# Hybrid diffusion backbone: the second choice of experts ahead of the first lowered piece, and the third piece behind the first hidden product

## Chip, cores, metric

One NeuronCore of a Trainium2 chip runs the whole program. The metric is the device time in microseconds (us), a median over several executions.

## What is computed

Two layers, each with a token mixer (neighbourhood attention, a Mamba-2 scan and a gated MLP) and a channel mixer, for 128 context tokens and 128 latent tokens with D = 1024. The change is in the channel mixer, a hierarchical mixture of experts with 4 groups of 8 experts, of which each token takes one group and two experts of it:

```python
p_coarse = jax.nn.softmax((x @ w_coarse).astype(jnp.float32), -1)
p_g, g_sel = lax.top_k(p_coarse, 1)
fine = (x @ w_fine).astype(jnp.float32).reshape(-1, MOE_GROUPS, MOE_EXPERTS_PER_GROUP)
fine_g = jnp.take_along_axis(fine, g_sel[:, :, None], axis=1)[:, 0]
top_v, top_i = lax.top_k(fine_g, MOE_TOP_K)
w_top = jax.nn.softmax(top_v, -1) * p_g
...
hid = jax.nn.silu(jnp.einsum('td,edf->tef', x, w1)) * jnp.einsum('td,edf->tef', x, w3)
y = jnp.einsum('tef,efd->td', hid * gates[:, :, None], w2)
```

## The kernel before

The five engines run instruction streams written out by hand, each in its own block, and meet at semaphores. An engine works through its stream in order, so the order in the text of a block is the order on the engine. `wait_ge` waits for a semaphore; `tally(ins, sem)` lets an instruction increment one, `drain()` on DVE or ACT is an instruction of the engine's queue that stands for the end of what came before it.

**Weights.** The weights of the experts come as pieces of 128 x 2048 fp32 (1 MB) in the order of `BODY` (line 81): piece 0 and 1 are the halves of `up` (w1 and w3) of expert 0, then for each further expert two pieces `up` and the piece `down` (w2) of the expert before. So piece 2 and 3 are `up` of expert 1, piece 4 is `down` of expert 0. SP loads piece j to slot j % 4 of `raw` once the slot is free (`expert_loads`). Each product is made in three matmuls (`mm3`) from a high and a low part of both factors: ACT copies a piece to `wh` (`convert`, L1691), DVE subtracts it from the piece to `wl` (`lower`, which is called `piece(j)` in the stream, L1792) and thereby gives back the slot. There are three pairs of buffers wh and wl (`PARTS = 3`), given back by TensorE.

**Routing.** From the logits DVE finds the coarse group (`first`, L2355) and the first choice of experts; TensorE counts ranks; DVE makes the selection matrix `selg` of group 0 (`choose(0, 0)`, L2363), which releases the gathers. Then DVE lowers piece 0 (`lower(Tally(dve), 0, 0)`). `finish_routing` finds the second choice, hands it to ACT for an exponential (`rt_in`; `grown(1)` on ACT, L1704), and makes the gates. ACT does the exponential for the group softmax (`grown(0)`) before its loop, and `grown(1)` after it has copied x2 to x2h (L1738).

**Entrance to the loop.** TensorE gathers the tokens of group 0 with 32 matmuls (gather 0 and gather 1, `bank<-selg,x`); ACT takes the high part (`xgh`, L1726) and DVE the low part (`xgl`). `up(0)` is 24 matmuls from `wh`, `wl`, `xgh`, `xgl`: its first half needs piece 0 and gather 0, its second half piece 1 and gather 1. Behind it gather 4 turns selg and picks the gates of the group; for that it waits for `gsel_ready`, the copy of the gates that `weigh` makes on DVE (L2430). DVE then copies the results (`gg`, L2456, `selT`, L2457) and makes `hid` of expert 0 (L2482) with ACT's `sil` (L1748). TensorE turns hid (L920), goes on to `up(1)`, whose first half needs piece 2, gathers a part of group 1 between its halves (this waits for `select(tally, rnd, 1)` on DVE), and does `down(0)` behind it.

**Loop.** For each expert DVE has: hid, piece 3i+3, the low part of the turned hid (`hTTl`), some extra work, pieces 3i+4 and 3i+5. ACT has: sil, piece 3i+3, `hTTh` (L1754), pieces 3i+4 and 3i+5. The order on DVE at the entrance was: gather 0's low part, piece 1, gather 1's low part, `finish_routing`, `weigh`, piece 2, the copies of gather 4.

The whole is done twice, for layer 0 and layer 1 (the entrances are at about 356 and 1011 us). A second round of the loop exists for groups of more than 128 tokens; it did not run here.

Of the kernel before, what the change touches and what calls it, by code (L numbers as in the profile page):

```python
# [342 lines left out]
def hybrid_backbone(nc, A, O):  # L343

    with ExitStack() as ctx:
# [1114 lines left out]
        def _(act):  # L1460
# [30 lines left out]
            for l in range(L):  # L1491
# [209 lines left out]
                def grown(n):  # L1701
                    act.wait_ge(rt_in, 2 * l + n + 1)
                    w = rtr[:, :, 0:4] if n == 0 else rtr[:, :, 40:41]
                    A_(w, w, ACT.Exp).then_inc(rt_exp, 1)  # L1704

                grown(0)

                def begin(tally, rnd):
                    if rnd:
                        convert(tally, rnd, 0)  # L1710

                def stream(tally, rnd, final):
                    def piece(j):
                        if j < len(BODY):
                            convert(tally, rnd, j)

                    def summed(g):
                        for n in range(2):
                            b = SUM_BANK + n
                            act.wait_ge(full[b], loop_uses(b, l, rnd, g + 1 - n))  # L1720
                            tally(A_(ygh[:, n * 512:(n + 1) * 512], bank[b][:, :], ACT.Copy), yg_high)

                    def gathered(g, j):
                        b, n = gather_use(g, j)
                        act.wait_ge(full[b], loop_uses(b, l, rnd, n))
                        ins = A_(xgh[g % 2][:, 4 * j:4 * j + 4, :], bank[b][:, :].rearrange("p (c t) -> p c t", c=4), ACT.Copy)  # L1726
                        if g:
                            ins.then_inc(free[b], 1)
                        tally(act.drain(), xg_act)

                    gathered(0, 0)
                    if rnd:
                        piece(1)
                    gathered(0, 1)
                    piece(2)
                    if rnd == 0:
                        for s in range(2):
                            A_(x2h[:, s, :], x2[:, s, :], ACT.Copy)  # L1738
                            act.drain().then_inc(x2_high, 1)
                        grown(1)  # L1740
                    for i in range(NE):
                        g, e = i // EPG, i % EPG
                        if i == NE - LATE:
                            tally.late = act.mark_branch_hint_location()
                        act.wait_ge(full[UP_BANK], loop_uses(UP_BANK, l, rnd, 1 + i))

                        act.wait_ge(free[UP_BANK], loop_uses(UP_BANK, l, rnd, 1 + i))
                        tally(A_(sil[:, :], bank[UP_BANK][:, 0:FF], ACT.Silu), sil_done)  # L1748
                        piece(3 * i + 3)
                        if i == NE - 1 and final and l < L - 1:  # L1750
                            cut[l + 1] = 0
                            convert_to(l + 1, 0)
                        act.wait_ge(full[TURN_BANK], loop_uses(TURN_BANK, l, rnd, TURN_USE["hidden", i]))
                        tally(A_(hTTh[i == NE - 1][:, :, :], bank[TURN_BANK][:, 0:FF].rearrange("p (c t) -> p c t", c=2), ACT.Copy), hidT_high)  # L1754
                        if i and e == 0:
                            summed(g - 1)
                        piece(3 * i + 4)
                        piece(3 * i + 5)
                        if i + 1 < NE and prepared_at(i + 1):
                            to, j = prepared_at(i + 1)  # L1760
                            if j < 2:
                                gathered(to, j)
                    summed(EG - 1)
                    if final and l < L - 1:
                        convert_to(l + 1, 1)
# [21 lines left out]
        def _(dve):  # L1787
# [81 lines left out]
            for l in range(L):  # L1869
# [472 lines left out]
                def r_(a, b):  # L2342
                    return rtr[:, :, a:b]
# [44 lines left out]
                V.tensor_scalar(place[:, :, 1:2], place[:, :, 0:1], -float(P), None, ALU.add)  # L2388
                bank_full(dve, l, "x211")
                choose(0, 0).then_inc(sel_ready, 1)  # L2390
                lower(Tally(dve), 0, 0)
                def finish_routing():

                    first(24, 8, "rev8", 5)
                    V.scalar_tensor_tensor(out=r_(16, 24), in0=r_(24, 32), scalar=-BIG, in1=r_(16, 24), op0=ALU.mult, op1=ALU.add)
                    drain()
                    V.tensor_reduce(r_(7, 8), r_(16, 24), X, ALU.max)
                    drain()
                    tt(r_(32, 40), r_(16, 24), r_(7, 8).to_broadcast([P, 2, 8]), ALU.is_equal)
                    tt(r_(40, 41), r_(7, 8), r_(6, 7), ALU.subtract)  # L2400
                    drain().then_inc(rt_in, 1)

                    first(32, 8, "rev8", 5)
                    dve.wait_ge(rt_exp, 2 * l + 2)
                    V.tensor_reduce(r_(41, 42), r_(0, 4), X, ALU.add)
                    V.tensor_scalar(r_(42, 43), r_(40, 41), 1.0, None, ALU.add)
                    drain()
                    tt(r_(43, 44), r_(41, 42), r_(42, 43), ALU.mult)
                    drain()
                    V.reciprocal(r_(44, 45), r_(43, 44))  # L2410
                    drain()
                    tt(r_(45, 46), r_(44, 45), r_(40, 41), ALU.mult)
                    drain()
                    tt(r_(24, 32), r_(24, 32), r_(44, 45).to_broadcast([P, 2, 8]), ALU.mult)
                    tt(r_(32, 40), r_(32, 40), r_(45, 46).to_broadcast([P, 2, 8]), ALU.mult)
                    drain()
                    tt(r_(24, 32), r_(24, 32), r_(32, 40), ALU.add)
                    drain()
                    for s in range(2):
                        tt(gates[:, s, :].rearrange("p (g e) -> p g e", g=4), bc(rtr[:, s, 24:32], 1, 4), bc(rtr[:, s, 8:12], 2, 8), ALU.mult)  # L2420
                    drain()

                def begin(tally, rnd):
                    if rnd:
# [12 lines left out]
                def stream(tally, rnd, final, begins=0, ends=NE):  # L2437
                    def piece(j):
                        if j < len(BODY):
                            lower(tally, rnd, j)  # L2440
# [26 lines left out]
                            tally(drain(), yg_low)  # L2467

                    if begins == 0:
                        gathered(0, 0)  # L2470
                        piece(1)
                        gathered(0, 1)
                        if rnd == 0:
                            finish_routing()
                            weigh(tally, 0)
                            piece(2)
                        gathered(0, 4)
                    for i in range(begins, ends):
                        g, e = i // EPG, i % EPG
# [2 lines left out]
                        tally(V.scalar_tensor_tensor(out=hid[:, :], in0=bank[UP_BANK][:, FF:2 * FF], scalar=gg[:, g % 2, e:e + 1],  # L2482
                                                     in1=sil[:, :], op0=ALU.mult, op1=ALU.mult), free[UP_BANK])
                        tally(drain(), hid_ready)
                        if i == 0 and rnd:
                            piece(2)
                        piece(3 * i + 3)
                        dve.wait_ge(full[TURN_BANK], loop_uses(TURN_BANK, l, rnd, TURN_USE["hidden", i]))
# [68 lines left out]
```

## Time and profile before

| | before |
|---|---|
| three runs | 1343.54, 1347.97, 1348.94 us |
| median | 1347.97 us |
| span of the profiled execution | 1351.2 us |
| TensorE busy | 1250.6 us (93%) |
| DVE busy | 1006.3 us (74%) |
| ACT busy | 741.8 us (55%) |
| HBM read | 349.77 MB, 262 GB/s over the span |

All rows come from that one execution of 1351.2 us. Busy shares are averages over stages of different kinds, so the stage in question has to be read by its own rows: who waited for whom there. A row of the timeline gives in brackets how long the engine was idle before the instruction and what ended it; "issue" means that the profile shows nothing it waited for. Matmul ends are modelled; starts are firmer.

### The profile page before, as it was taken

The numbers are of one execution on the slowest core, as the hardware profiler recorded it, in microseconds if no ns is written. First come the engines' busy times: TensorE is split into PE (matmuls) and PEld (weight loads), VectorE is DVE, ScalarE is ACT, GpSimd is POOL, SyncE is SP. The second block draws the span as 40 slices with busy tenths as digits, with TensorE's granted clock in tenths as the row PEclk, the third lists the DMA queues.
The fourth block names the chain that finished last, engine by engine and source line by source line (L and its number), as shares of the span: only waits on it lengthen the run. The fifth ranks groups of instructions, "written<-read, shape, count | busy, mean of one in ns | idle before, by whom it ended". The sixth has DMA issues, their size and how long they took to land.

```text
span 1351.2 us, 16800 instructions
## 1 busy us (share of the span) xinstructions
PE 1250.6 (93%) x6097; PEld 977.0 (72%) x6097; DVE 1006.3 (74%) x1154; ACT 741.8 (55%) x704; POOL 66.8 (5%) x113
## 2 busy tenths in 40 slices
PE   4999999989899999999989999998988999999994
PEld 1767777777676777887757777776777778788773
DVE  0646567787589888888877475768857888888886
ACT  1543453652656667677753345356346566666773
POOL 1400001001000000000020000010000000000000
PEclk8899998989889999999989989998999999999998
DMA  9988654538668989899976767454436898889991
GB/s 357 315 271 312 247 176 138 185 108 327 238 250 315 336 313 344 316 339 343 354 216 206 276 231 268 156 171 149 156 130 225 282 361 324 319 328 337 340 355 56
DMA packets 98092, 353.68 MB, mean 262 GB/s; under 512 B 9060, under 2 KB 12608, under 8 KB 81616
## 3 DMA queue, kind: packets, MB, share of 16 engines
q1 hardware_dynamic: 87504, 295.12, 61.0%
q0 software_dynamic: 10496, 57.39, 12.3%
q8 instruction: 51, 0.84, 0.2%
q14 instruction: 41, 0.34, 0.1%
HBM read 349.77 MB, written 3.74 MB: 262 GB/s over the span
## 4 chain that ended last, share of the span: by engine, by line
PE 60%; DVE 23%; ACT 5%; DMA 5%; issue 3%; DVEq 3%; ACTq 1%; SPq 1%; POOL 0%; POOLq 0%
PE bank L917 56%; DVE wl L1792 13%; PE bank L920 3%; DMA adaw<-in_w_ada 2%; ACT wh L1691 2%; DMA first<-in_w_ada 1%; DVE tmp L1792 1%; ACT wh L1484 1%; DVE merged L1792 1%; DVE hid L2482 1%; DMA decay<-decay_rows 1%; DVE x L1792 1%; ACTq L1579 1%; DMA raw<-in_moe_w 1%; ACT gate L1578 0%
## 5 line engine op out<-in xcount | busy, mean ns | idle before, releaser
L1792 DVE TENSOR_TENSOR wl<-raw,wh 128x2048 fp32r<-128x2048 f32 (+1 forms) x268 | 610.4, 2278 | 126.2 <-ACT wh L1484 78.8
L1691 ACT ACTIVATE wh<-raw 128x2048 fp32r<-128x2048 f32 x192 | 367.6, 1917 | 60.3 <-PE bank L917 50.9
L917 PE MATMUL bank<-wh,xgh 128*128 128x512 f32 x512 | 211.6, 413 | 0.1
L917 PE MATMUL bank<-wh,xgl 128*128 128x512 f32 x512 | 204.3, 399 | 0.0
L917 PE MATMUL bank<-wl,xgh 128*128 128x512 f32 x512 | 203.8, 398 | 0.0
L1484 ACT ACTIVATE wh<-raw 128x2048 fp32r<-128x2048 f32 (+1 forms) x76 | 142.3, 1872 | 103.8 <-PE bank L917 62.7
L917 PE MATMUL bank<-wh,hTh 128*128 128x512 f32 x448 | 186.4, 416 | 6.9 <-DVE wl L1792 4.0
L917 PE MATMUL bank<-wl,hTh 128*128 128x512 f32 x448 | 181.7, 406 | 0.0
L917 PE MATMUL bank<-wh,hTl 128*128 128x512 f32 x448 | 181.0, 404 | 0.0
L917 PEld LDWEIGHTS bank<-wh,xgl 128*128 128x128 f32 x512 | 97.3, 190 | 23.6
L917 PEld LDWEIGHTS bank<-wh,xgh 128*128 128x128 f32 x512 | 98.0, 191 | 20.0 <-issue 0.5
L917 PEld LDWEIGHTS bank<-wl,xgh 128*128 128x128 f32 x512 | 97.9, 191 | 19.7
L917 PEld LDWEIGHTS bank<-wh,hTh 128*128 128x128 f32 x448 | 87.3, 195 | 30.9 <-DVE wl L1792 7.7
L917 PE MATMUL bank<-wh,hTTh 128*128 128x512 f32 x256 | 102.7, 401 | 2.5 <-DVE wl L1792 2.5
L917 PEld LDWEIGHTS bank<-wh,hTl 128*128 128x128 f32 x448 | 87.0, 194 | 21.4
L917 PEld LDWEIGHTS bank<-wl,hTh 128*128 128x128 f32 x448 | 87.5, 195 | 19.4
L917 PE MATMUL bank<-wl,hTTh 128*128 128x512 f32 x256 | 101.5, 396 | 0.0
L917 PE MATMUL bank<-wh,hTTl 128*128 128x512 f32 x256 | 101.3, 396 | 0.0
L1754 ACT ACTIVATE hTTh<-bank 128x256 fp32r<-128x256 f32 x64 | 24.7, 386 | 86.5 <-PE bank L920 86.5
L917 PEld LDWEIGHTS bank<-wh,hTTh 128*128 128x128 f32 x256 | 48.2, 188 | 18.1 <-DVE wl L1792 6.4
L1748 ACT ACTIVATE sil<-bank 128x256 f32<-128x256 f32 x64 | 24.6, 385 | 59.7 <-PE bank L917 59.7
L917 PEld LDWEIGHTS bank<-wh,hTTl 128*128 128x128 f32 x256 | 48.2, 188 | 11.7
(302 smaller groups left out, 1563.6 us busy)
## 6 DMA issues: line engine op xcount, KB each, us to landing
raw<-in_moe_w SPq DMA_DIRECT2D x256, 512.0 KB, 4.7
raw<-in_moe_w SPq DMA_DIRECT2D x64, 1024.0 KB, 5.2
raw<-in_w_in SPq DMA_DIRECT2D x52, 1024.0 KB, 6.1
adaw<-in_w_ada POOLq DMA_DIRECT2D x32, 1024.0 KB, 6.4
raw<-in_w_branch SPq DMA_DIRECT2D x12, 1024.0 KB, 5.2
raw<-in_w_ada SPq DMA_DIRECT2D x8, 1024.0 KB, 10.6
raw<-in_w_o SPq DMA_DIRECT2D x8, 1024.0 KB, 4.8
first<-in_w_ada SPq DMA_DIRECT2D x4, 1024.0 KB, 16.8
```

Source lines behind the costliest of these rows:

```text
L917: return behind(nc.tensor.matmul(*args, **kw))
L920: return behind(nc.tensor.transpose(*args))
L1484: A_(wh[c][:, 0:n], raw[:, r, 0:n], ACT.Copy).then_inc(part_high[c], 1)
L1579: act.drain().then_inc(gate_ready, 1)
L1691: tally(A_(wh[c][:, :], raw[:, r, :], ACT.Copy), part_high[c])
L1748: tally(A_(sil[:, :], bank[UP_BANK][:, 0:FF], ACT.Silu), sil_done)
L1754: tally(A_(hTTh[i == NE - 1][:, :, :], bank[TURN_BANK][:, 0:FF].rearrange("p (c t) -> p c t", c=2), ACT.Copy), hidT_high)
L1792: return V.tensor_tensor(o, a, b, op)
L2482: tally(V.scalar_tensor_tensor(out=hid[:, :], in0=bank[UP_BANK][:, FF:2 * FF], scalar=gg[:, g % 2, e:e + 1], in1=sil[:, :], op0=ALU.mult, ...
```

## The change

The seven operations on DVE that find the second choice leave `finish_routing` and become `second_choice`, which runs before piece 0 is lowered. `grown(1)` on ACT runs directly behind `grown(0)`. In the stream on DVE, piece 1 stands ahead of the low part of gather 0, and piece 2 behind hid of expert 0 (ahead of piece 3), as it already stood in a second round. The operations are the same; none is added or removed.

```diff
--- before.py
+++ after.py
@@ -1704,6 +1704,7 @@
                     A_(w, w, ACT.Exp).then_inc(rt_exp, 1)
 
                 grown(0)
+                grown(1)
 
                 def begin(tally, rnd):
                     if rnd:
@@ -1737,7 +1738,6 @@
                         for s in range(2):
                             A_(x2h[:, s, :], x2[:, s, :], ACT.Copy)
                             act.drain().then_inc(x2_high, 1)
-                        grown(1)
                     for i in range(NE):
                         g, e = i // EPG, i % EPG
                         if i == NE - LATE:
@@ -2388,8 +2388,8 @@
                 V.tensor_scalar(place[:, :, 1:2], place[:, :, 0:1], -float(P), None, ALU.add)
                 bank_full(dve, l, "x211")
                 choose(0, 0).then_inc(sel_ready, 1)
-                lower(Tally(dve), 0, 0)
-                def finish_routing():
+
+                def second_choice():
 
                     first(24, 8, "rev8", 5)
                     V.scalar_tensor_tensor(out=r_(16, 24), in0=r_(24, 32), scalar=-BIG, in1=r_(16, 24), op0=ALU.mult, op1=ALU.add)
@@ -2399,6 +2399,8 @@
                     tt(r_(32, 40), r_(16, 24), r_(7, 8).to_broadcast([P, 2, 8]), ALU.is_equal)
                     tt(r_(40, 41), r_(7, 8), r_(6, 7), ALU.subtract)
                     drain().then_inc(rt_in, 1)
+
+                def finish_routing():
 
                     first(32, 8, "rev8", 5)
                     dve.wait_ge(rt_exp, 2 * l + 2)
@@ -2419,6 +2421,9 @@
                     for s in range(2):
                         tt(gates[:, s, :].rearrange("p (g e) -> p g e", g=4), bc(rtr[:, s, 24:32], 1, 4), bc(rtr[:, s, 8:12], 2, 8), ALU.mult)
                     drain()
+
+                second_choice()
+                lower(Tally(dve), 0, 0)
 
                 def begin(tally, rnd):
                     if rnd:
@@ -2467,13 +2472,12 @@
                             tally(drain(), yg_low)
 
                     if begins == 0:
+                        piece(1)
                         gathered(0, 0)
-                        piece(1)
                         gathered(0, 1)
                         if rnd == 0:
                             finish_routing()
                             weigh(tally, 0)
-                            piece(2)
                         gathered(0, 4)
                     for i in range(begins, ends):
                         g, e = i // EPG, i % EPG
@@ -2482,7 +2486,7 @@
                         tally(V.scalar_tensor_tensor(out=hid[:, :], in0=bank[UP_BANK][:, FF:2 * FF], scalar=gg[:, g % 2, e:e + 1],
                                                      in1=sil[:, :], op0=ALU.mult, op1=ALU.mult), free[UP_BANK])
                         tally(drain(), hid_ready)
-                        if i == 0 and rnd:
+                        if i == 0:
                             piece(2)
                         piece(3 * i + 3)
                         dve.wait_ge(full[TURN_BANK], loop_uses(TURN_BANK, l, rnd, TURN_USE["hidden", i]))
```

## Rows read from the trace of the kernel before

**Rows 1.** The page's chain that ended last, shares of the span by line
```profile
PE bank L917 56%; DVE wl L1792 13%; PE bank L920 3%; DMA adaw<-in_w_ada 2%; ACT wh L1691 2%; DMA first<-in_w_ada 1%; DVE tmp L1792 1%; ACT wh L1484 1%; DVE merged L1792 1%; DVE hid L2482 1%; DMA decay<-decay_rows 1%; DVE x L1792 1%; ACTq L1
```

**Rows 2.** Chain of work from 384 to 446 us, shares by line
```profile
by line: DVE wl L1792 62.9%; DVE x L1792 7.9%; issue 6.9%; DVE hTTl L1792 4.1%; DVE x2l L1792 4.0%; DVE hid L2482 3.9%; ACT wh L1691 3.1%; DVE xgl L2453 2.2%; DVEq L2334 1.3%; DVE selg L2363 0.6%; DVEq L2458 0.5%; DVEq L2492 0.5%; DVEq L236
```

**Rows 3.** Timeline of DVE, layer 0: start us, us, engine, line, op, out<-in, [idle before <-releaser]
```profile
356.00 2.29 DVE L1792 TENSOR_TENSOR wl<-raw,wh 128x2048 fp32r<-128x2048 f32 x1
360.73 0.69 DVE L1792 TENSOR_TENSOR xgl<-bank,xgh 128x512 fp32r<-128x512 f32 x1 [2.43 <-ACTq L1729]
361.55 2.29 DVE L1792 TENSOR_TENSOR wl<-raw,wh 128x2048 fp32r<-128x2048 f32 x1
364.05 0.69 DVE L1792 TENSOR_TENSOR xgl<-bank,xgh 128x512 fp32r<-128x512 f32 x1 [0.20 <-issue]
364.88 0.18 DVE L1792 TENSOR_TENSOR rtr<-rtr,cst 128x16 f32<-128x16 f32 x1
...
366.50 0.17 DVE L1792 TENSOR_TENSOR rtr<-rtr,cst 128x16 f32<-128x16 f32 x1
...
368.04 0.16 DVE L2405 TENSOR_REDUCE rtr<-rtr 128x2 f32<-128x8 f32 x1 [0.87 <-ACT rtr L1704]
...
370.02 0.17 DVE L2430 COPY gsel<-gates 128x16 f32<-128x16 f32 x1
...
373.45 0.48 DVE L2482 SCALAR_TENSOR_TENSOR hid<-bank,gg,sil 128x256 f32<-128x256 f32 x1 [0.21 <-issue]
...
376.57 0.42 DVE L1792 TENSOR_TENSOR hTTl<-bank,hTTh 128x256 fp32r<-128x256 f32 x1 [0.20 <-issue]
...
385.95 2.29 DVE L1792 TENSOR_TENSOR wl<-raw,wh 128x2048 fp32r<-128x2048 f32 x1 [1.17 <-ACT wh L1691]
```

**Rows 4.** Timeline of TensorE (PE), layer 0
```profile
362.63 0.48 PE L917 MATMUL bank<-wh,xgh 128*128 128x512 f32 x1
...
370.37 0.41 PE L920 MATMUL bank<-cst,selg 128*128 128x128 f32 x2 [1.89 <-DVEq L2431]
370.61 0.51 PE L917 MATMUL bank<-gsel,selg 128*128 128x8 f32 x4
...
374.13 0.67 PE L920 MATMUL bank<-cst,hid 128*128 128x128 f32 x2 [1.14 <-DVEq L2484]
...
380.35 0.44 PE L917 MATMUL bank<-wh,xgh 128*128 128x512 f32 x1
```

**Rows 5.** Timeline of ACT, layer 0
```profile
357.75 0.21 ACT L1704 ACTIVATE rtr<-rtr 128x8 f32<-128x8 f32 x1
...
383.99 1.92 ACT L1691 ACTIVATE wh<-raw 128x2048 fp32r<-128x2048 f32 x1 [0.20 <-issue]
```

**Rows 6.** Timeline of DVE, layer 1
```profile
1030.84 0.60 DVE L2363 TENSOR_SCALAR selg<-cst,place,rtr 128x128 fp32r<-128x128 f32 x2
...
1038.58 2.29 DVE L1792 TENSOR_TENSOR wl<-raw,wh 128x2048 fp32r<-128x2048 f32 x1 [0.90 <-ACT wh L1691]
```

**Rows 7.** Timeline of TensorE (PE), layer 1
```profile
1010.86 5.38 PE L917 MATMUL bank<-selg,x 128*128 128x128 f32 x32 [2.21 <-DVEq L2365]
1016.21 0.47 PE L917 MATMUL bank<-wh,xgh 128*128 128x512 f32 x1
...
1024.08 0.41 PE L920 MATMUL bank<-cst,selg 128*128 128x128 f32 x2 [1.65 <-DVEq L2431]
...
1027.83 0.67 PE L920 MATMUL bank<-cst,hid 128*128 128x128 f32 x2 [3.00 <-DVEq L2484]
...
1033.27 0.45 PE L917 MATMUL bank<-wh,xgh 128*128 128x512 f32 x1
```

**Rows 8.** Windows: stretch, us, busy us of PE, PEld, DVE, ACT, POOL, then PEclk, DMA, GB/s
```profile
372.40:379.20 6.80, 5.66 (x16) 4.62 (x17) 5.48 (x14) 2.19 (x2) 0.00 (x0) 0.50 0.68 234
...
1012.00:1013.00 1.00, 1.00 (x7) 1.00 (x7) 1.00 (x1) 0.00 (x0) 0.00 (x0) 0.50 0.00 0
...
1027.80:1031.20 3.40, 3.37 (x9) 2.81 (x10) 3.05 (x4) 2.19 (x2) 0.00 (x0) 0.50 0.81 290
```

## Prediction

> **What bounds the kernel now.** I read the page's chain first: matmuls of the helper line 917 are 56% of the span and the low parts of the weights on DVE (line 1792) 13% [rows 1]. TensorE sets the time in most of the program. The change sits where each layer goes from routing to the expert loop (layer 0 from 355.9 us, layer 1 from 1010.8 us), so I read the timelines of the engines there, and then the chain behind it. From 384 to 446 us of layer 0 the chain lies on DVE, 62.9% of it on pieces of weights alone [rows 2]: early experts are tied to DVE's order, and a DVE that comes out of the entrance earlier takes the chain with it.
>
> In layer 0, DVE lowers piece 0 at 356.00, then waits 2.43 us for the first gather (360.73), lowers piece 1, takes the second gather's low part (364.05) and only then starts on the second choice (364.88 to 366.50), the gates (to 370.02, with 0.87 us of wait for the exponential), piece 2, the copies of gather 4 and hid of expert 0 (373.45) [rows 3]. TensorE waits for this three times: it ends up(0) at 370.37 - 1.89 = 368.48 and waits 1.89 us for gsel, then 1.14 us for hid [rows 4]. In layer 1 these waits are 1.65 and 3.00 us [rows 7]. They are what the change can win: 3.03 and 4.65 us.
>
> **Second choice earlier.** Nothing is added or removed: seven small DVE operations take 366.50 - 364.88 = 1.62 us [rows 3] and move ahead of piece 0. There they fall into the 2.43 us of idle time, but push piece 0 to 356.00 + 1.62 = 357.62.
>
> **Piece 1 ahead of the first gather.** A piece with the gap behind it is 364.05 - 361.55 = 2.50 us [rows 3]. So piece 0 ends about 360.1, piece 1 at 362.6, and the low part of gather 0 starts at 362.6 instead of 360.73 and is ready (0.69 us and a drain) at 363.4. TensorE started up(0) at 362.63 [rows 4], so it now waits 0.8 us more. That is the price in layer 0. In layer 1 the gathers ran faster and up(0) began at 1016.21 [rows 7]; there DVE starts at 1010.9, piece 0 runs from 1012.5, piece 1 from 1015.0, the low part from 1017.5, and up(0) can begin at 1018.3: 2.1 us later.
>
> **Exponential on ACT.** It moves directly behind the first one (357.75) [rows 5]. ACT now waits at the head of its queue for the second choice, with the copy of gather 0 queued behind; DVE got that copy at 360.73, so it began about as long before as DVE's own pass takes, at 360.0. The choice is there at 357.6, the exponential of 0.21 us ends at about 358.2, so 1.8 us are left; the order is the same in layer 1. I price it at nothing; if this cover were gone, each microsecond would delay xgh. Its removal behind x2h takes away the 0.87 us of DVE idle [rows 3]. No other function comes between the two exponentials, so I add no table load.
>
> **Gates and gather 4.** Without the second choice and the wait, from the second xgl to gsel ready is 370.02 - 366.50 - 0.87 = 2.65 us plus 0.3 for gsel. Layer 0: xgl of gather 1 is ready at about 364.5, gsel at 367.5. Layer 1: 1019.1 and 1022.1. up(0) lasts 368.48 - 362.63 = 5.85 us [rows 4] (6.22 in layer 1 with a stall of 0.3 between its halves [rows 7], which goes, since both low parts are ready). It ends at 369.25 and 1024.15, after gsel in both. **The first wait is gone, and TensorE is last.**
>
> **Piece 2 behind hid.** From gsel's copy to hid were 3.43 us [rows 3], of which 0.29 is gsel and 2.43 the piece: 0.71 remain for the copies of gather 4. Gather 4 is 0.75 us on TensorE [rows 4]. So hid starts at 369.25 + 0.75 + 0.1 + 0.7 = 370.8 and is handed over at 371.4, against 374.1: 2.7 us earlier. Layer 1: 1025.7 and 1026.3, against 1027.8. But now piece 2 is lowered behind hid, and up(1) needs it: ready at 373.85 in layer 0, at 1028.75 in layer 1. up(1) started just behind the turns of hid (374.13 and 1027.83, plus 0.32 us). **So the second wait isn't closed: it becomes a wait for piece 2 between the turns and up(1).** Layer 0 is 0.6 us ahead there, layer 1 is 0.6 us behind.
>
> Queued behind piece 2 on DVE are piece 3, the low part of hid turned and the choice for group 1. In layer 0 the low part comes at 376.35 against 376.57 [rows 3]; in layer 1 the choice comes at about 1031.8 against 1030.84 [rows 6]. Slot 2 of the raw weights is given back about 1.1 and 2.4 us later, so SP issues piece 6 later, by 373.8 and 1028.7; ACT took it only at 383.99 in layer 0 [rows 5], so I count no cost. Piece 4 in slot 0 goes 1.6 us later and piece 5 in slot 1 1.2 to 1.5 us earlier; both are wanted over 10 us later.
>
> **What is left of it at the second piece of expert 1.** Layer 0: from 374.45 to the second half of up(1) at 380.35 [rows 4] were 5.9 us, of which 4.75 at the lower clock level (0.50, 1.2 GHz, from 372.4 to 379.2 [rows 8]). Work at half clock counts half, so it is 2.37 + 1.15 = 3.52 us of full clock (2.4 GHz). From 373.85 on, with the clock low to 379.2 again, 2.67 of it are done by then and the rest by 380.05: 0.3 us sooner. With a low stretch of 3.4 us, as layer 1 had, it is 373.85 + 3.4 + 1.82 = 379.1: 1.3 us sooner. And with less of it still, DVE, whose pieces 4 and 5 move by only 0.2, can start piece 6 no earlier than 384.6 against 385.95 (1.17 us idle there [rows 3]): at most 1.35 us. I take 1.0, nearer to the layer 1 case, since after the change layer 0 too has one gap there where it had two. Layer 1: up(1) starts 0.6 later, in a low stretch of 1027.8 to 1031.2 [rows 8]; by the same count the way to its second half at 1033.27 [rows 7] was 1.52 + 2.07 = 3.59 us of full clock; from 1028.75, 1.22 are done at 1031.2 and the rest at 1033.6. The choice of group 1 is ready at 1032.5, just ahead of its gather. That is 0.3 us late, and DVE's 0.90 us idle at piece 6 [rows 6] covers its own delay. I keep +0.1 (no low stretch, but the choice waited for) to +0.6.
>
> **Sum:** -1.0 + 0.3 = -0.7 us; bounds from -1.35 + 0.1 = -1.25 to -0.3 + 0.6 = +0.3. Against the profiled span of 1351.2 us it gives 1350.5. That execution was 3.2 us above the median 1347.97; the edit is a shift of two entrances, so the same 0.7 comes off the median: 1347.3 us. The loop behind waits for its own slots, so I let the shift last to the end.
>
> **Rivals.**
>
> A, the clock falls in the new gap (ends slower). In layer 1, TensorE idles 1016.2 to 1018.3, right ahead of the dense up(0). A gap of 2.21 us at 1010.86 [rows 7] was followed by 0.50 [rows 8], and even the one of 1.14 us in layer 0 by a low stretch. Against it: over 5 us of gathers stand before it. A low stretch of 3.4 us at half rate costs 1.7 us, all on TensorE's own path. It decides if the matmuls of up(0) start 0.43 us apart: -0.7 + 1.7 = +1.0, 1349.0 us; with another in layer 0, 1350.7.
>
> B, the clock stays up throughout the entrance. Layer 0 then gains its full 1.35, layer 1 loses 0.1: 1346.7 us. The trace speaks against it with both low stretches [rows 8]. The Trainium skill ("TensorE: Matmul & The Clock Gate", Why this matters for your kernels) has it that only a long idle gap between bursts of matmuls sets the clock back. By that rule B would hold, since the new gaps are at most 2.1 us; but here the trace differs, with a low level behind an idle time of 1.14 us.
>
> C, the reorder only moves waits: the wait for piece 2 swallows both gains and a later wait of the loop (DVE's chain to 446 us, or a load) takes the rest. 1348.0 us. For it: the loop's engines are within tenths of each other in these stretches, DVE carrying the chain.
>
> **How the numbers follow.** Forecast 0.40, A 0.25, B 0.20, C 0.15. All four lie within 0.5% (6.7 us), which is about what a measurement of this kernel can tell from no change, and even all waits closed (3.03 + 4.65 = 7.7 us) would only just pass it. The runs of before reach from 1343.54 to 1348.94, so the median of a few can lie some microseconds off; moved by the cases this gives 1342.5 to 1350.5. Faster by over 0.5%: 0.05; within: 0.91; slower: 0.04.
>
> **What would show it.** Right: no wait of TensorE for gsel; a new one for xgl ahead of up(0), 0.8 us in layer 0 and 2.1 in layer 1; hid of expert 0 about 2.7 and 1.5 us sooner after the choice; a new wait of TensorE for piece 2, about 1.5 to 2.2 us; the exponentials 0.3 us apart on ACT. Wrong: xgh delayed by ACT's wait; low clock under up(0); gsel later than up(0)'s end; or a start of expert 1 in layer 1 that isn't later.

## Result: slower by 0.3 to 0.5%

The changed kernel takes 1355.78 us in the median against 1348.45 us of the kernel before, a ratio of 1.0046 (95% interval 1.0029 to 1.0062). Two later measurements of it gave 1.0029 (1.0011 to 1.0048) and 1.0036 (1.0020 to 1.0051). So it loses 4 to 6 us, 5 in the mean of the three ratios. I had forecast 1347.3 us, a gain of 0.7 us, with 1350.5 us as the upper end.

The page of the changed kernel, the lines that answer to the table of before and to [rows 1] (busy us and share of each engine, then the chain that ended last by engine and by line). The busy times of TensorE, DVE and ACT are the same to 0.4 us, the span is 3.9 us longer, and the chain has 2 to 3% less of TensorE and 1% more of DVE's pieces:

```profile
span 1355.1 us, 16797 instructions
...
PE 1251.0 (92%) x6094; PEld 976.2 (72%) x6097; DVE 1006.6 (74%) x1154; ACT 741.4 (55%) x704; POOL 67.1 (5%) x113
...
PE 57%; DVE 25%; DMA 5%; ACT 4%; issue 3%; DVEq 3%; ACTq 1%; SPq 1%; POOL 0%; POOLq 0%
PE bank L917 54%; DVE wl L1792 14%; PE bank L920 3%; DVE tmp L1792 1%; ACT wh L1691 1%; DMA first<-in_w_ada 1%; ACT wh L1484 1%; DMA raw<-in_moe_w 1%; DMA decay<-decay_rows 1%; DMA adaw<-in_w_ada 1%; DVE merged L1792 1%; DVE hid L2486 1%; DVE x L1792 1%; ACTq L1579 1%; DVEq L2281 0%
```

The timeline of DVE at the entrance of layer 0, answering to [rows 3] (columns as there; the choice of group 0 ends at 357.16 here and at 355.9 before, so subtract 1.3 us to compare):

```profile
357.27 0.17 DVE L1792 TENSOR_TENSOR rtr<-rtr,cst 128x16 f32<-128x16 f32 x1
...
358.88 2.29 DVE L1792 TENSOR_TENSOR wl<-raw,wh 128x2048 fp32r<-128x2048 f32 x1
361.40 2.29 DVE L1792 TENSOR_TENSOR wl<-raw,wh 128x2048 fp32r<-128x2048 f32 x1 [0.23 <-issue]
363.90 0.69 DVE L1792 TENSOR_TENSOR xgl<-bank,xgh 128x512 fp32r<-128x512 f32 x1 [0.21 <-issue]
...
368.37 0.17 DVE L2435 COPY gsel<-gates 128x16 f32<-128x16 f32 x1
372.97 0.17 DVE L2461 COPY gg<-bank 128x8 f32<-128x8 f32 x1 [4.43 <-PE bank L917]
...
373.68 0.48 DVE L2486 SCALAR_TENSOR_TENSOR hid<-bank,gg,sil 128x256 f32<-128x256 f32 x1 [0.21 <-issue]
374.30 4.72 DVE L1792 TENSOR_TENSOR wl<-raw,wh 128x2048 fp32r<-128x2048 f32 x2
```

The second choice, the two pieces and the first low part follow each other without a wait, as forecast. The new thing is the row at 372.97: DVE has gsel ready at 368.54 and then has **nothing to do for 4.43 us**, until TensorE is through with up(0) and gather 4. Piece 2, which stood there before, now comes behind hid.

TensorE at the same place, answering to [rows 4]:

```profile
357.45 3.81 PE L917 MATMUL bank<-selg,x 128*128 128x128 f32 x32 [2.08 <-DVEq L2365]
364.98 0.47 PE L917 MATMUL bank<-wh,xgh 128*128 128x512 f32 x1 [3.72 <-DVEq L2455]
...
366.24 0.63 PE L917 MATMUL bank<-wh,xgl 128*128 128x512 f32 x1
...
372.21 0.38 PE L920 MATMUL bank<-cst,selg 128*128 128x128 f32 x2
...
376.74 0.77 PE L917 MATMUL bank<-wh,xgh 128*128 128x512 f32 x1 [1.63 <-DVE wl L1792]
```

It waits 3.72 us ahead of up(0) (I had said 0.8, for in the profile of before the gathers took 6.66 us, part of them at the lower clock, and ended late; here they took 3.81), none for gsel (372.21), and 1.63 us for piece 2 (376.74). Layer 1, answering to [rows 7], and DVE there, answering to [rows 6]:

```profile
1010.43 5.47 PE L917 MATMUL bank<-selg,x 128*128 128x128 f32 x32 [2.21 <-DVEq L2365]
1018.07 0.71 PE L917 MATMUL bank<-wh,xgh 128*128 128x512 f32 x1 [2.18 <-DVEq L2455]
...
1025.30 0.38 PE L920 MATMUL bank<-cst,selg 128*128 128x128 f32 x2
...
1027.46 0.48 PE L920 MATMUL bank<-cst,hid 128*128 128x128 f32 x2 [1.43 <-DVEq L2488]
1029.84 0.77 PE L917 MATMUL bank<-wh,xgh 128*128 128x512 f32 x1 [1.90 <-DVE wl L1792]
...
1035.99 0.45 PE L917 MATMUL bank<-wh,xgh 128*128 128x512 f32 x1
```

```profile
1017.08 0.69 DVE L1792 TENSOR_TENSOR xgl<-bank,xgh 128x512 fp32r<-128x512 f32 x1 [0.20 <-issue]
...
1021.55 0.18 DVE L2435 COPY gsel<-gates 128x16 f32<-128x16 f32 x1
1026.07 0.17 DVE L2461 COPY gg<-bank 128x8 f32<-128x8 f32 x1 [4.34 <-PE bank L917]
...
1037.42 2.29 DVE L1792 TENSOR_TENSOR wl<-raw,wh 128x2048 fp32r<-128x2048 f32 x1 [1.22 <-ACT wh L1691]
```

Again 2.18 us ahead of up(0), 4.34 us of DVE idle, 1.90 us of TensorE for piece 2. The windows of 1 us, in the columns of [rows 8], show the clock at its lower level (0.50) under up(0) and again under up(1), in layer 0 and in layer 1:

```profile
367.00:368.00 1.00, 1.00 (x4) 0.72 (x4) 0.70 (x6) 0.49 (x1) 0.00 (x0) 0.50 0.93 381
...
378.00:379.00 1.00, 1.00 (x3) 0.73 (x3) 1.00 (x1) 0.00 (x0) 0.00 (x0) 0.50 0.80 295
```

```profile
1020.00:1021.00 1.00, 1.00 (x4) 0.81 (x3) 0.70 (x6) 0.86 (x2) 0.00 (x0) 0.50 0.96 373
...
1031.00:1032.00 1.00, 1.00 (x4) 0.81 (x3) 1.00 (x1) 0.00 (x0) 0.00 (x0) 0.50 0.95 344
```

**Where the time is.** Take as marks the row of the need flag (L2384, just ahead of the choice of group 0) and the rows of hid. In layer 1 the flag and hid of expert 4, first before, then after:

```profile
1009.26 0.14 DVE L2384 TENSOR_SCALAR need<-rank 1x1 int32<-1x1 f32 x1
...
1070.74 0.48 DVE L2482 SCALAR_TENSOR_TENSOR hid<-bank,gg,sil 128x256 f32<-128x256 f32 x1 [0.21 <-issue]
```

```profile
1008.82 0.14 DVE L2384 TENSOR_SCALAR need<-rank 1x1 int32<-1x1 f32 x1
...
1073.44 0.48 DVE L2486 SCALAR_TENSOR_TENSOR hid<-bank,gg,sil 128x256 f32<-128x256 f32 x1 [0.20 <-issue]
```

From the flag to hid of expert 4 the two layers took 63.78 and 61.48 us before, and 64.14 and 64.62 us after: 3.5 us of the 3.9 by which the two spans differ. Three more profiled executions of each kernel give 125.8, 124.2 and 124.0 us for the sum of before (125.3 in the first) and 125.7, 128.3 and 126.7 us after (128.8 in the first): means of 124.8 and 127.4, **2.6 us more**. From hid of expert 4 to hid of the last expert the two layers together take the same (512.8 us before, 513.0 after, in the means of four). The stages ahead of the two flags, which no edit touches, differ by 5 us and more from one profiled execution of one kernel to the next (683.2 to 688.5 us before, 681.1 to 691.2 after, 1.0 us more in the mean). So the four spans differ by 3.8 us in the mean, of which 2.6 lie in the entrances; the median times differ by about 5. Whether the part outside the entrances belongs to the change or to chance stays open.

### The profile page after: what moved, and what is told of

The parts are those of the page before. It is cut to its first block, busy times and chain, and to the rows that moved or that the text cites. A ratio compares the mean times of both kernels' runs of the same rounds, so it can differ in the third digit from the quotient of the medians.

```text
span 1355.1 us, 16797 instructions
## 1 busy us (share of the span) xinstructions
PE 1251.0 (92%) x6094; PEld 976.2 (72%) x6097; DVE 1006.6 (74%) x1154; ACT 741.4 (55%) x704; POOL 67.1 (5%) x113
## 4 chain that ended last, share of the span: by engine, by line
PE 57%; DVE 25%; DMA 5%; ACT 4%; issue 3%; DVEq 3%; ACTq 1%; SPq 1%; POOL 0%; POOLq 0%
PE bank L917 54%; DVE wl L1792 14%; PE bank L920 3%; DVE tmp L1792 1%; ACT wh L1691 1%; DMA first<-in_w_ada 1%; ACT wh L1484 1%; DMA raw<-in_moe_w 1%; DMA decay<-decay_rows 1%; DMA adaw<-in_w_ada 1%; DVE merged L1792 1%; DVE hid L2486 1%; DVE x L1792 1%; ACTq L1579 1%; DVEq L2281 0%
## 5 line engine op out<-in xcount | busy, mean ns | idle before, releaser
L1691 ACT ACTIVATE wh<-raw 128x2048 fp32r<-128x2048 f32 x192 | 367.5, 1917 | 66.4 <-PE bank L917 52.9
L1484 ACT ACTIVATE wh<-raw 128x2048 fp32r<-128x2048 f32 (+1 forms) x76 | 142.4, 1873 | 103.2 <-PE bank L917 62.3
L917 PEld LDWEIGHTS bank<-wh,xgl 128*128 128x128 f32 x512 | 98.0, 191 | 23.9
L917 PEld LDWEIGHTS bank<-wl,hTh 128*128 128x128 f32 x448 | 87.9, 196 | 19.5
```

What stands on the lines that cost most here:

```text
L917: return behind(nc.tensor.matmul(*args, **kw))
L1484: A_(wh[c][:, 0:n], raw[:, r, 0:n], ACT.Copy).then_inc(part_high[c], 1)
L1691: tally(A_(wh[c][:, :], raw[:, r, :], ACT.Copy), part_high[c])
```

## Experiments

All ratios are to the kernel before, timed beside it on the same chip, with 95% intervals. "Entrance" is the time from the need flag to hid of expert 4, layer 0 and layer 1, in the profile of that kernel.

### Only one of the two pieces moved back

```diff
--- changed kernel, DVE
+++ first experiment
-                        piece(1)
                         gathered(0, 0)
+                        piece(1)
```

> The changed kernel with piece 1 again behind the low part of gather 0 (second choice early, piece 2 late as in the change). Theory G (the gap ahead of up(0) and the low clock behind it make the loss): TensorE's idle time ahead of up(0) falls from 2.2 to 3.7 us to 1.5 us at most, up(0) runs at full clock, and the time is 1348 to 1350 us, most of the 6 us back. Theory P (piece 2 behind hid makes it, through its own gap and the low clock under up(1)): the gap of 1.6 to 1.9 us ahead of up(1) stays, and the time is 1353 to 1355. Theory M (the loss lies outside the entrances): no change, 1355.

Ratio 0.9987 (0.9971 to 1.0003), 1348.82 us; entrance 61.6 and 61.2 us. TensorE started up(0) without a wait behind the gathers, at full clock, and waited 1.62 and 1.71 us for piece 2. The loss is gone, as theory G said, although the wait for piece 2 stayed.

```diff
--- changed kernel, DVE
+++ second experiment
                             weigh(tally, 0)
+                            piece(2)
                         gathered(0, 4)
...
-                        if i == 0:
+                        if i == 0 and rnd:
                             piece(2)
```

> The changed kernel with piece 2 again ahead of the copies of gather 4 (second choice early, piece 1 early as in the change). DVE is idle for over 4 us there, so the piece costs hid nothing. Theory G: the gap ahead of up(0) and its low clock stay (about 3 us per layer), but the wait for piece 2 goes, 1.6 to 1.9 us per layer: 1351 to 1353. Theory P: all of the loss goes, 1346 to 1349. Theory M: 1355.

Ratio 0.9981 (0.9962 to 1.0000), 1346.73 us; entrance 60.7 and 59.5 us. Here the gap ahead of up(0) stayed (0.72 and 2.23 us), up(0) was as late as in the changed kernel, and the loss was gone all the same. So the late start of up(0) alone doesn't make the loss, as theory G wanted (the low clock under up(0), its other half, did not come in this profile), and P fits no better, since the first experiment kept piece 2 late. **Behind the early second choice each piece may be moved without the other; only both together lose.** (Both pieces moved without the early choice was not run.) DVE in layer 1 of the second experiment shows what differs:

```profile
1017.50 0.17 DVE L2435 COPY gsel<-gates 128x16 f32<-128x16 f32 x1
1017.79 2.29 DVE L1792 TENSOR_TENSOR wl<-raw,wh 128x2048 fp32r<-128x2048 f32 x1
1020.49 0.17 DVE L2461 COPY gg<-bank 128x8 f32<-128x8 f32 x1 [0.41 <-PE bank L917]
...
1021.21 0.48 DVE L2487 SCALAR_TENSOR_TENSOR hid<-bank,gg,sil 128x256 f32<-128x256 f32 x1 [0.22 <-issue]
```

Piece 2 (1017.79) lies in the time in which TensorE is still at up(0), and only 0.41 us of DVE's wait for gather 4 are left, where the changed kernel has 4.34. That comparison holds at full clock too: in another profiled execution of the changed kernel (the one under "The changed kernel again") up(0) also ran at full clock and began at the same 8.9 and 9.3 us behind the flag as in the second experiment, and yet its entrances were 5.5 us longer in sum. Its DVE in layer 1:

```profile
1024.22 0.18 DVE L2435 COPY gsel<-gates 128x16 f32<-128x16 f32 x1
1027.21 0.17 DVE L2461 COPY gg<-bank 128x8 f32<-128x8 f32 x1 [2.81 <-PE bank L917]
```

### The second choice alone

> Only the second choice ahead of piece 0 and its exponential behind the first; piece 1 and piece 2 where they were before. Theory G: the low part of gather 0 comes up to 1.4 us later where the gathers run at full clock, hardly at all where they run at the lower one; gsel comes 1.0 to 1.6 us earlier, and with it hid: 1345 to 1348 us, no slower than the kernel before. Theory P: the same, 1345 to 1348. If the early choice itself is the cause: 1351 or more.

Ratio 0.9982 (0.9966 to 0.9997), 1346.45 us; entrance 60.1 and 59.4 us, in the profile 5.8 us shorter in sum than the first of before (5.3 than the mean of its four), while the time is only 2.4 us shorter. DVE in layer 1:

```profile
1006.94 2.29 DVE L1792 TENSOR_TENSOR wl<-raw,wh 128x2048 fp32r<-128x2048 f32 x1
1009.52 0.69 DVE L1792 TENSOR_TENSOR xgl<-bank,xgh 128x512 fp32r<-128x512 f32 x1 [0.28 <-issue]
...
1016.70 2.29 DVE L1792 TENSOR_TENSOR wl<-raw,wh 128x2048 fp32r<-128x2048 f32 x1
1019.13 0.17 DVE L2461 COPY gg<-bank 128x8 f32<-128x8 f32 x1
...
1019.84 0.48 DVE L2487 SCALAR_TENSOR_TENSOR hid<-bank,gg,sil 128x256 f32<-128x256 f32 x1 [0.22 <-issue]
```

From the choice of group 0 to hid DVE has hardly a gap: the second choice (1.6 us) fills the wait for the first gather of [rows 3], and piece 2 fills the wait for gather 4.

These three and the changed kernel are all four combinations of the two moves behind the early choice: 0.9982 with neither, 0.9981 with piece 1 alone, 0.9987 with piece 2 alone, and 1.0029 to 1.0046 with both. The early choice gains, and the two moves together cost some 7 us of it.

### An account of DVE

This gave a theory that the first three didn't have, **theory D**: the entrance is DVE's. Add up the idle times of DVE from the need flag to hid of expert 1, and take them from the whole stretch. The rest is DVE's own work, and the same to 0.5 us in all profiles of a layer, as it must be if every version does the same operations:

| kernel | flag to hid 1, layer 0 / 1 | DVE idle | rest |
|---|---|---|---|
| before, first profile | 29.58 / 27.94 | 4.13 / 3.87 | 25.4 / 24.1 |
| changed, first profile | 30.97 / 31.10 | 5.70 / 7.28 | 25.3 / 23.8 |
| piece 1 back | 28.40 / 27.65 | 2.97 / 3.70 | 25.4 / 23.9 |
| piece 2 back | 27.24 / 26.38 | 2.13 / 2.60 | 25.1 / 23.8 |
| choice alone | 26.65 / 25.89 | 1.11 / 1.85 | 25.5 / 24.0 |

The sum is bookkeeping and would come out for any engine; what it adds is where the difference sits: in which wait of DVE a piece lies or does not lie. In these profiles a piece put into a wait of DVE lengthened the entrance little, and a piece taken out of one left the wait empty, wherever TensorE stood. The four profiles of the changed kernel have 13.0, 8.6, 11.3 and 9.7 us of idle time in the two layers together, those of before 8.0, 8.8, 7.3 and 6.8: 2.9 us more in the mean, about the 2.6 us that the entrances are longer.

That the entrances decide the time is borne out by all 14 ratios of this document taken together. In the order of the ratios, from 0.9959 to 1.0046, the sums of the two entrances are 119.1, 119.2, 120.2, 119.5, 122.8, 122.0, 125.8, 125.8, 121.5, 126.1, 126.3, 125.7, 128.3 and 128.8 us. Each sum is of one profiled execution. One stands clearly out of the order, the 121.5 us of piece 1 alone.

### Is it the clock?

The next expectations speak of a theory I: the two moved pieces spoil each other, since piece 1 opens a gap ahead of up(0) and the delay can't be made up while piece 2 waits behind hid. To test the clock's part, matmuls in bf16 whose product nobody reads were put on a free bank, in the gaps of TensorE (`warm(n)` issues n of them, 128x512 each). First 8 ahead of up(0):

```diff
--- changed kernel, TensorE
+++ with matmuls ahead of up(0)
...
                     for j in range(2):
                         gather(tally, rnd, 0, j)
+                    if rnd == 0:
+                        warm(8)
```

> The changed kernel with 8 matmuls of 128x512 in bf16 on a free bank behind the gathers, ahead of up(0), whose product nobody reads; they fill about 1.7 us of the gap. Theory G with the clock as its larger part: up(0) runs at full clock in both layers, up(0) ends 1.4 to 1.7 us sooner per layer, and the time is 1351 to 1353 us. If only the length of the gap counts and not the clock: no change or up to 1 us slower, 1355 to 1357.

Ratio 1.0023 (1.0008 to 1.0039), 1352.6 us; up(0) ran at full clock in both layers, but under up(1) the clock was low again for 8 and 12 matmuls. 1352.6 us lies in the range written for the clock as the larger part, though the interval lets anything from a fifth of the loss to the whole of it be left. Then also 8 ahead of up(1), and 5 behind gather 4 in layer 1:

> The changed kernel with idle stretches of TensorE filled by bf16 matmuls nobody reads: 8 ahead of up(0), 8 between the turns of hid and up(1), and in layer 1 also 5 behind gather 4. The waits for DVE stay as they are. Theory I with the clock as the cause of most of the loss: up(0) and up(1) run at the higher clock, hid of expert 4 comes at 60.5 to 62 us behind the need flag in both layers, 1348 to 1350 us. If the waits themselves are the loss: no gain over the changed kernel, 1353 to 1356.

Ratio 1.0024 (1.0012 to 1.0036), 1353.6 us, in the range written for the waits as the loss; entrance 64.1 and 62.2 us. up(1) ran at full clock in both layers, but in layer 1 the added matmuls themselves pushed up(0) from 9.25 to 9.7 us behind the flag, and in layer 0 the gathers were so fast that a gap of 1.90 us stayed and up(0) fell to the lower level for 8 matmuls all the same. DVE's wait at the copies of gather 4 in that layer:

```profile
372.76 0.17 DVE L2478 COPY gg<-bank 128x8 f32<-128x8 f32 x1 [4.33 <-PE bank L917]
```

With up(1) at full clock the result is still slower than before. The clock lengthens the wait (4.33 to 4.43 us with up(0) low, 2.8 to 2.9 with up(0) high and nothing pushed), but **most of the wait is there at full clock too**. up(0) ends 1.5 to 1.6 us later where it falls to the lower level, which was in 3 of the 8 entrances of the changed kernel: 1.2 us for an execution, of the 2.6 by which the entrances are longer. So of the loss against the kernel before, the clock under up(0) is nearly half in the profiles, and the timed runs (1.0023 and 1.0024 against 1.0029 to 1.0046) can't part it more sharply. Of the 7 us against the choice alone it is the smaller part in these profiles.

### The changed kernel again, and piece 2 alone

> The changed kernel itself once more, as the mark for the others and as a second look at the clock. Theory I (the two moved pieces spoil each other: piece 1 opens a gap ahead of up(0), up(0) then runs at the lower clock and ends late, and the delay cannot be made up because piece 2 waits behind hid): again a gap of 2 to 4 us ahead of up(0) in both layers, low clock under up(0) in at least one layer, hid of expert 4 at 62 to 65 us behind the need flag, and 1352 to 1356 us. Rival N (the measured loss was a chance of the clock's phase and of the mixer stages): the entrances come out as in the runs with one piece moved back, 60 to 61.5 us, and 1349 to 1351.

Ratio 1.0029; gaps of 2.20 and 2.02 us ahead of up(0), but no low clock under it in either layer: this part of my expectation was wrong. Entrance 63.7 and 62.0 us. Under up(1) the clock was low for 12 and 7 of its first 12 matmuls.

> Only piece 2 moves behind hid; second choice and piece 1 as before. Theory I: TensorE still waits for gsel (1.6 to 1.9 us), then hid comes about 2.4 us sooner and up(1) waits for piece 2; nothing ahead of up(0) changes, so the result is near the kernel before, 1347 to 1351. Theory P (piece 2 behind hid loses by itself): 1352 or more.

Ratio 1.0012 (0.9996 to 1.0028), 1351.29 us; entrance 62.3 and 63.5 us. Near the kernel before, as theory I said; with 5.70 us of DVE idle in layer 1 there is no gain in it.

### Piece 1 alone, and the choice at another place

> Only piece 1 moves ahead of the low part of gather 0; the second choice and piece 2 as before. Theory D (from the need flag to hid of expert 1 DVE has the same work in every version, 24.0 to 24.4 us in layer 1 and 25.1 to 25.8 in layer 0, and the entrance lasts this work plus DVE's idle time): piece 1 fills the 2.0 to 2.4 us in which DVE waited for the gather, so the gap ahead of up(0) costs nothing. Left is a wait for the exponential of 1 to 1.5 us, which now comes later on ACT than DVE wants it. Hid of expert 1 at 26.5 to 27.3 us in layer 1 (27.94 before), 1346 to 1349 us in all. Theory G (a later up(0) costs what it is late): hid of expert 1 at 29 us or more in layer 1, 1351 or more.

In layer 0 hid of expert 1 came at 26.7 us with 1.4 us of idle time; in layer 1 at 27.76 us, later than I expected, because the wait for the exponential was there and two smaller ones beside it:

```profile
1015.41 0.16 DVE L2405 TENSOR_REDUCE rtr<-rtr 128x2 f32<-128x8 f32 x1 [1.28 <-ACT rtr L1704]
```

The work without the idle was 23.85 us, about what theory D wants, but the ratio was 1.0013 (0.9996 to 1.0029), 1350.78 us, though this profile's entrances are 3.8 us shorter in sum than those of before's first. One profiled execution doesn't rank versions that lie 2 or 3 us apart; this one contradicts the timing, which gives theory D no support here, and I can't say why.

```diff
--- second choice alone
+++ second choice behind piece 0
-                second_choice()
                 lower(Tally(dve), 0, 0)
+                second_choice()
```

> As the third experiment (second choice early, pieces 1 and 2 as before), but the choice stands behind piece 0, inside the wait for the gather, instead of ahead of it. Theory D: DVE's idle time is the same either way, so hid of expert 1 comes at 26.0 to 26.8 us in layer 0 and 25.7 to 26.2 in layer 1, and the time is that of the third experiment, 1345 to 1348. If an earlier piece 0 or the later choice matters, it differs by over 1 us per layer.

Ratio 0.9989 (0.9971 to 1.0006); hid of expert 1 at 28.1 and 27.3 us, 1.4 us later than with the choice ahead of piece 0 and outside what I expected. ACT in layer 1 shows the reason:

```profile
1003.86 0.21 ACT L1704 ACTIVATE rtr<-rtr 128x8 f32<-128x8 f32 x1
1006.46 0.21 ACT L1704 ACTIVATE rtr<-rtr 128x2 f32<-128x2 f32 x1 [2.39 <-DVEq L2401]
1007.23 0.60 ACT L1727 ACTIVATE xgh<-bank 128x512 fp32r<-128x512 f32 x1 [0.56 <-issue]
```

ACT waited 2.39 us at the head of its queue for the choice and its high part of gather 0 (xgh) came only at 1007.23; DVE then idled 1.55 us for it. This is the cover of 1.8 us that the prediction named: with the choice 2.4 us later it is gone, and the wait that I had priced at nothing costs. That speaks for the place ahead of piece 0, but only in one profile: the two ratios (0.9989 and 0.9982) don't tell the places apart.

### A faster version

The choice alone, with bf16 matmuls in TensorE's idle time ahead of the turns of hid (1.14 and 3.00 us in [rows 4, 7]), on the bank that the turns then use:

```diff
--- second choice alone, TensorE
+++ with matmuls ahead of the turns
+                            if rnd == 0:
+                                loop_free(rnd, TURN_BANK, TURN_USE["hidden", 0])
+                                masks = cst[:, P:3 * P].bitcast(BF16)
+                                for _ in range(5 if l < L - 1 else 12):
+                                    mm(bank[TURN_BANK][:, :], masks[:, 0:P], masks[:, 0:512], start=True, stop=True, skip_group_check=True)
```

> Only the second choice early (the third experiment), plus bf16 matmuls nobody reads in the idle stretch of TensorE ahead of the turns of hid of expert 0: 5 in layer 0, 12 in layer 1. If the low clock under up(1) is worth its price there, up(1) runs at the higher clock and hid of expert 1 comes 0.5 to 1.0 us sooner per layer, 1344 to 1346 us. If DVE sets the pace there, no change, 1346 to 1348.

> The fastest version once more (second choice early, matmuls nobody reads ahead of the turns of hid of expert 0). If the first measurement holds, the ratio to the kernel before is 0.995 to 0.998, 1342 to 1346 us; if its gain over the third experiment was chance, 0.998 to 0.999.

Ratios 0.9959 (0.9941 to 0.9977) and 0.9970 (0.9955 to 0.9985), 1343.87 and 1345.29 us: faster than the kernel before by 4 to 5.5 us, in both. TensorE in layer 1 of the first:

```profile
1018.05 2.75 PE L917 MATMUL bank<-cst 128*128 128x512 bf16 x12
1021.20 0.47 PE L920 MATMUL bank<-cst,hid 128*128 128x128 f32 x2 [0.40 <-DVEq L2494]
1021.43 0.47 PE L917 MATMUL bank<-wh,xgh 128*128 128x512 f32 x1
1021.74 0.40 PE L917 MATMUL bank<-wl,xgh 128*128 128x512 f32 x1
```

The 12 matmuls end 0.40 us before the turns, up(1) starts at full clock (0.40 us a matmul, not 0.63), and the entrance of layer 1 is 58.9 us in both profiles, 0.5 us less than with the choice alone. But what I had expected did not come: hid of expert 1 is at 26.67 and 25.79 us in the first of the two profiles, against 26.65 and 25.89 with the choice alone, and not 0.5 to 1.0 us sooner. In layer 0 the 5 matmuls were followed by 7 low ones under up(1) in the first profile and by none in the second. The entrances account for 0.3 to 0.4 us, and the intervals overlap with that of the choice alone (0.9966 to 0.9997), so **it is not shown that the added matmuls gain anything over the early choice**; shown is that the two together beat the kernel before.

### The control and the last profiles

> The kernel before, unchanged, as a control and for a second look at its entrances: ratio 1.000 within the interval. Theory D: hid of expert 1 again at work plus idle, with 3.3 to 4.0 us of DVE idle time, the wait for the first gather the largest of it; where the gathers run at the higher clock the wait shrinks and the entrance of layer 0 is 1 to 2 us shorter than in the first profile.

Ratio 0.9996 (0.9981 to 1.0012). DVE idle 4.40 and 4.38 us, a little above what I had expected, the wait for the first gather 2.43 and 1.20 us. Its gathers of layer 0 ran at the lower clock as in the first profile.

> The changed kernel, third look. If the entrances carry the loss, their sum is 127 to 130 us in most looks at it (DVE idle of 2.8 to 4.4 us ahead of the copies of gather 4 in both layers, the longer one where up(0) runs at the lower clock); if they carry only a part, it is near 126 and the mixer stages are longer. Ratio again 1.002 to 1.005.

> The kernel before, third look: sum of the entrances 124 to 126.5 us, DVE idle before the first low part 1.2 to 2.4 us in each layer.

> The changed kernel, fourth look: sum of the entrances 127 to 130 us if they carry the loss, near 126 if they carry only a part of it.

> The kernel before, fourth look: sum of the entrances 124 to 126.5 us, as in its three other looks.

Changed: 128.3 and 126.7 us (the second lies between the two cases that I had written down), ratio 1.0036 in the timed one. Before: 124.2 and 124.0 us. In these two the gathers of layer 0 ran faster (up(0) at 6.7 us behind the flag instead of 7.9) and the entrance of layer 0 took 62.4 us instead of 63.8: the profile that I predicted from showed the slower of two courses.

## Why the prediction was wrong

**Up to the start of up(1) the steps held.** Measured from the need flag, I had put up(1) at 19.1 us in layer 0 and 19.5 in layer 1 after the change; the four profiles have 19.1 and 19.5 wherever up(0) ran at full clock, and 20.7 to 21.0 where it did not. The wait for gsel went, the wait for hid shrank, the wait for piece 2 took its place, the exponentials ran behind each other under cover: all as written.

**The step that failed is "What is left of it at the second piece of expert 1".** I had the second half of up(1) 1.0 us earlier in layer 0 and 0.3 us later in layer 1. In the means of four profiles it is 1.0 us later in layer 0 (26.0 against 25.0 us behind the flag) and 1.5 us later in layer 1 (25.7 against 24.2). That is 2.5 us later instead of 0.7 us earlier, and nearly the whole 2.6 us of the entrances. The 3.2 us between are made of three terms:

1. **The low clock under up(1), 1.6 us.** I let the low stretch end where it had ended before, or be 3.4 us long, so that the way from the start of up(1) to its second half took 5.5 and 4.85 us. It took 6.1 and 5.8 us, with no wait in it. In all 8 entrances of the changed kernel the level fell within the new wait for piece 2, 17.8 to 20.2 us behind the flag (15.8 to 18.6 in the kernel before), and 7 to 12 of the 12 matmuls in the first half of up(1) were low. I had also misread the rows: in layer 0 of before the low stretch begins at 372.4 us, during the narrow matmuls (128x8) that end at 372.99, and so ahead of the idle time of 1.14 us behind which rivals A and B place it.
2. **The low clock under up(0), 1.2 us.** It is rival A, left out of the forecast; it came in 3 of 8 entrances with 1.5 to 1.6 us each.
3. **The profile I started from, 0.4 us.** In layer 0 it showed slow gathers; in two of four profiles of before the same point was at 24.2 to 24.3 us already, and not at 25.6. In layer 1 it was 0.2 us early.

A smaller slip is without effect: the two low parts behind each other are given 1.9 us in layer 0 and 1.6 us in layer 1, and took 1.6 us in both; gsel was ready before the end of up(0) either way.

**Why there was nothing to win.** I followed TensorE. The prediction itself says that the chain from 384 us on is DVE's [rows 2], and it moves a piece of 2.4 us out of a stretch in which, by its own times, DVE has gsel ready at 367.5 and nothing to do before gather 4 at 370.0. I never summed DVE's idle time: 2.43 + 0.87 us taken away, 2.5 us and more added. The second choice and piece 1 both went into one wait of 1.2 to 2.4 us that could hold one of them at most; the rest pushed up(0) out, and the longer wait for up(0) was then left empty. The runs with one piece moved back show that this empty wait is what undoes the gain of the early choice.

**Rival A** (+1.7 us for the low clock in one layer, 1350.7 us with it in both) is real in size. In the first profile it came in both layers, yet the time was 5 us above its price. **Rival C**, that the reorder only moves waits, is nearest to the rest of the mechanism; I had priced it at no change. **Rival B** was not tested: with up(1) at full clock in both layers the kernel was still at 1.0024, but up(0) fell in one of them.

The range was too low because each case was priced by itself, at 1.7 us a layer at most, and none allowed them to add. Its upper end of 1350.5 us even lies below the 1350.7 us of my own rival A. And about half of the measured loss isn't placed at all: the entrances carry 2.6 of the 5 us, and the rest stays open.

## What to carry to other kernels

Before moving a step, write for the engine that carries the chain all its waits over the stretch, with their lengths, and see which piece lies in which wait. Here the sum of these waits followed the length of the entrances to about half a microsecond; the time of the whole program followed them in its order, but not in each step. A wait can hide only as much as it is long, so two steps moved into the same wait are priced together, not one by one. And look at more than one execution before taking a gain of one microsecond from a stretch where the clock changes level.

## What the runs showed of the hardware

The same idle time of TensorE is followed by the lower clock level in one execution and not in another. The gap ahead of up(0) in the changed kernel was followed by it at 3.72, 2.18 and 2.00 us, and not at 2.20, 2.11, 2.02, 0.99 and 0.96 us, nor at 2.23 us in the second experiment and 1.99 us with piece 1 alone. The fall can also come late: behind the gap of 3.72 us, up(0) began at full clock at 364.98 and its matmuls were low only from 366.24 on. In the gap of 1.6 to 1.9 us ahead of up(1), with a few small matmuls and a further wait before it, the level fell in all 8 entrances. In layer 0 of the kernel before it fell in all four profiles during eight matmuls of 128x8 that ran for 2.01 us behind a wait of 1.9 us. In layer 1 of the faster version 2.75 us of bf16 matmuls whose product nobody reads, ending 0.40 us before the work, were followed by the higher level under up(1) in both profiles; but up(1) ran at it without them too in layer 1 of the second experiment. The Trainium skill ("TensorE: Matmul & The Clock Gate", Why this matters for your kernels) ties the fall to a long idle gap, which I had read as longer than the new gaps; here it followed a gap of 2.00 us behind 5.43 us of gathers, and came amid the narrow matmuls, so the measurement decides.

From the start of the span to the need flag of layer 0, which is the same code in every kernel here, it took 352.3 to 357.1 us over the profiled executions. That is as much as the whole effect under study, and it bounds what a single profile can say.
